# Norm factor applied behind the products: four MLPs, four FFNs and two cross-attention query products of a two-block network

## The chip, the cores and the metric

The kernel runs on one core of one Trainium2 chip. The metric is the device time of one launch in microseconds (us); lower is better. The engines are TensorE (PE in the rows, with its weight loads as PEld), VectorE (DVE), ScalarE (ACT), GpSimd (POOL) and SyncE (SP), which issues the weight transfers.

## The reference, cut to what matters

Every stage of the network starts with a norm of the residual x (256 tokens, 1024 channels) and ends by adding to x:

```
def rms_norm(x, g):                      # y = x * r * g, one factor r for each token
    y = x * lax.rsqrt(jnp.mean(x * x, axis=-1, keepdims=True) + 1e-6)
    return y * g

# block 1, four layers: mixer (gated delta rule, mLSTM, differential attention, gated delta rule), then
h = rms_norm(x, norm_g[i, 2])
x = x + rms_norm(jnp.square(jax.nn.relu(h @ w1)) @ w2, norm_g[i, 3])      # 1024 -> 4096 -> 1024

# block 2, two layers
x = x + 0.5 * swiglu(rms_norm(x, ffn1_norm), w_gate, w_up, w_down)        # 1024 -> 2816 -> 1024
x = x + hybrid_mixer(rms_norm(x, mix_norm), ...)
x = x + memory_cross_attention(rms_norm(x, cross_norm), rms_norm(mem, mem_norm), wq, wk, wv, wo)
x = x + 0.5 * swiglu(rms_norm(x, ffn2_norm), ...)
# swiglu(h) = (silu(h @ w_gate) * (h @ w_up)) @ w_down ; cross attention: q = h @ wq
```

## The kernel before

**Layout and products.** x is held transposed in xT (channels on partitions, 8 chunks of 128 channels by 256 tokens). All products are float32 made of three float32r products: an operand is split into a rounded high part and the rest as a low part, and high x high, high x low and low x high are summed in PSUM. Activations are split into hH and hL (the MLP's hidden ones into hidH and hidL), weights into wH and wL.

**Weights as slabs.** All weights come as 400 slabs of 1 MB (128 x 2048 float32) through a ring of 3 buffers. SP may load slab n when slab n-3 has its low part. ACT makes wH (`split`, L1058), DVE makes wL from it (L1495); there are two places for split slabs, so wH of slab n waits until the products of slab n-2 are done. A slab costs TensorE 48 matmuls of 256 columns (all at L459). On ACT, `ready(name, layer, j)` is the place in the queue where slab j+2 is split: it makes sure of the splits up to j+1, waits for the products of slab j, and splits slab j+2. On DVE `refill(name, layer, j)` makes wL up to slab j+2.

**Start of a stage.** DVE writes xT in four steps of two chunks (`post_norm`, L1534 and L1537, behind the four mixers of block 1 and its MLPs; `residual`, L1544, in block 2). ACT squares each step into sq (L1081), PE sums the squares over the channels with a matrix of ones (`norm_sum`, 8 matmuls in plain float32), ACT turns the sum into r by Ln and Exp (`rsqrt`, L1075 and L1076), DVE writes hT = x * g * r (L1506), ACT rounds it to hH (L1092), DVE makes hL (L1511), and `first_products` takes the stage's first two slabs together: for each pair of chunks of hH the first slab's high and low weights and the second slab's high weights, then hL, then the second slab's low weights. The third slab follows by `to_channels` or the loop in `ffn`. `ln_exp` (L1071) loads the activation table with Ln and Exp, at the head of ACT's part of a stage.

**The stages concerned.** `mlp` (4 times): 16 slabs of w1, each evacuated by ACT's Relu (L1141) and a DVE product of Relu and bank (L1560), split again to hidH and hidL, then 16 slabs of w2 and `post_norm`, which norms the product and adds it to x. `ffn` (4 times): 22 slabs with gate and up side by side; ACT's Silu of the gate half (L1159), DVE's product with the up half (L1582), hidH by ACT (L1154), hidL by DVE, then 11 slabs of w_down and `residual`. `cross` (2 times): 4 slabs of wq, evacuated by ACT's `channels` (L1121), while the memory is normed (in layer 0 with its own norm sum behind the third slab; the squares of the memory are L1414), then wk, wv, attention, wo.

The mlp stages and the first ffn start behind a `post_norm`, for which both slabs of the new stage have their wH already; the other five start behind a `residual`, where only the first slab has it, and ACT makes wH of the second slab behind the squares.

Of the kernel before, what the change touches and what calls it, by code (L numbers as in the profile page):

```python
# [15 lines left out]
P = 128  # L16
# [4 lines left out]
EPS = 1e-6  # L21
RING = 3
# [69 lines left out]

def schedule():
# [42 lines left out]

LAMBDA_INIT = 0.8 - 0.6 * math.exp(-0.3 * 2)


def program(nc, io, out, parts=None):  # L140
# [23 lines left out]
    with ExitStack() as ctx:  # L164
# [62 lines left out]
        with nc.sbuf_tensor("hidden_parts", [P, 2, 32, T], F32R) as hidden_parts:  # L227
            hidH, hidL = hidden_parts[:, 0, :, :], hidden_parts[:, 1, :, :]
        arena = sb("arena", [P, ARENA])
# [24 lines left out]
        prod_s = A.take(2 * 512, "p (b n) -> p b n", b=2)  # L254

# [36 lines left out]
        memH, memL = hidden_parts[:, 0, 24:32, :], hidden_parts[:, 1, 0:8, :]  # L292
        A = Arena(lay)
# [74 lines left out]
        def _(pool):  # L368
            scope[0] = ""
            W = Waits(pool, "pool_step")  # L370
            pool.memset(ones[:, :], 1.0)
            pool.memset(epsc[:, :], EPS).then_inc(sem("ones_set"), 1)
# [81 lines left out]
        def _(pe):  # L454
# [36 lines left out]
            def first_products(name, layer, js, c, at):  # L491
# [3 lines left out]
                high_w = [high(n[0], c), high(n[1], c)]  # L495
# [3 lines left out]
                def both_halves(b, w, x, k, ends=False):  # L499
                    for m in range(2):  # L500
                        ins = mm(ps[:, 4 + b, m * T:(m + 1) * T], at(w, k, m), x[:, k, :],
                                 w is high_w[b] and x is hH and k == 0 and m == 0, ends and k == DC - 1 and m == 1,
# [3 lines left out]
                for k0 in range(0, DC, 2):  # L506
                    pe.wait_ge(sem("hH_ready"), W.next("hH_ready"))
                    for b, w in ((0, high_w[0]), (0, low_w[0]), (1, high_w[1])):
                        for k in (k0, k0 + 1):
                            both_halves(b, w, hH, k)  # L510
                for k in range(DC):
                    if k % 2 == 0:
                        pe.wait_ge(sem("hL_ready"), W.next("hL_ready"))
                    last = both_halves(0, high_w[0], hL, k, ends=True)
                last.then_inc(sem("products_done"), 1)
                for k in range(DC):
                    both_halves(1, high_w[1], hL, k)
                pe.wait_ge(sem("low_split"), n[1] + 1)
                for k in range(DC):
                    last = both_halves(1, low_w[1], hH, k, ends=True)  # L520
# [29 lines left out]
            def norm_sum(bank=7):  # L550

                for c in range(4):
                    pe.wait_ge(sem("sq_ready"), W.next("sq_ready"))
                    for k in (2 * c, 2 * c + 1):
                        last = mm(ps[:, bank, 0:T], ones[:, 0:P], sq[:, k, :], k == 0, k == DC - 1)
                last.then_inc(sem("ss_ready"), 1)

# [28 lines left out]
            def down_product(name, layer, chunks, waited):  # L586

                for j in range(chunks // 2):
                    n = slab_no[(name, layer, j)]
# [17 lines left out]
            def mlp(i):  # L607
                norm_sum()
                first_products("mlp_w1", i, (0, 1), DC, columns)
                for j in range(2, 16):  # L610
                    to_channels("mlp_w1", i, j, bank_of(j), free="bank_read")
                down_product("mlp_w2", i, 32, range(0, 32, 2))
                pe.wait_ge(sem("bank_read"), W.next("bank_read", 4))
                norm_sum()

            def ffn(kind, l):
                norm_sum()
                first_products(kind, l, (0, 1), 2 * DC, lambda w, k, half: w[:, half * DC + k, :])
                for n in range(2, 22):
# [4 lines left out]
                    for half in range(2):  # L624
                        last = three(ps[:, 4 + n % 4, half * T:(half + 1) * T],
                                     [lambda k: wh[:, half * DC + k, :], lambda k: wl[:, half * DC + k, :]],
                                     [lambda k: hH[:, k, :], lambda k: hL[:, k, :]], DC,
# [325 lines left out]
            def cross(l):  # L953
                norm_sum()
# [4 lines left out]
                to_channels("cross_wq_2", l, 3, bank_of(3))  # L959
                pe.wait_ge(sem("mem_split"), W.next("mem_split", 4))  # L960
                for s in range(4):
                    pe.wait_ge(sem("evac"), W.next("evac"))
# [62 lines left out]
            pe.wait_ge(sem("lambda_ready"), W.next("lambda_ready"))  # L1025
            mm(ps[:, 1, 0:1], ones[0:1, 0:P], lwork[:, 130:131], True, True).then_inc(sem("lambda_spread"), 1)
            pe.wait_ge(sem("params_ready"), W.next("params_ready"))
# [7 lines left out]
            pe.wait_ge(sem("h_ready"), DC * (len(parts) + 1))  # L1035
# [8 lines left out]
        def _(act):  # L1044
# [28 lines left out]
            def rsqrt(src, dst, n, name):  # L1073

                W.chain(f(dst, src, ACT.Ln, scale=1.0 / n, bias=epsc[:, :]))  # L1075
                f(dst, dst, ACT.Exp, scale=-0.5).then_inc(sem(name), 1)  # L1076

            def norm(src, there, ahead):
# [5 lines left out]
                rsqrt(ps[:, 7, 0:T], rs[:, :], D, "rs_ready")  # L1084
# [8 lines left out]

            def split_mix(n):
# [5 lines left out]
            def post_norm(product):  # L1100

                norm(lambda c: two(ps[:, c, :]), lambda c: ready(*product(c), ahead=c < 3),
                     slab_no[product(3)[0:3]] + PARTS + 1)
# [33 lines left out]
            def mlp(i):  # L1137
                x_norm("mlp_w1", i)
# [6 lines left out]
                post_norm(lambda c: ("mlp_w2", i, 15, c))  # L1145
# [5 lines left out]
            def ffn(kind, l):  # L1151
                def hidden_high(n):
                    act.wait_ge(sem("bank_read"), W.next("bank_read"))
# [255 lines left out]
            def cross(l):  # L1409
                x_norm("cross_wq_2", l)  # L1410
# [5 lines left out]
                channels("cross_wq_2", l, 0, 4, chunks(qk, 0), scale=0.0625)  # L1416
# [7 lines left out]
                channels("cross_wq_2", l, 1, 6, chunks(qk, 4), scale=0.0625)  # L1424
# [38 lines left out]
            act.wait_ge(sem("lambda_sums"), W.next("lambda_sums"))  # L1463
            f(lwork[:, 130:132], lwork[:, 128:130], ACT.Exp).then_inc(sem("lambda_exp"), 1)
# [531 lines left out]
```

## Time and profile before

| | us |
|---|---|
| median of 3 runs | 3054.18 |
| the three runs | 3053.6, 3054.18, 3063.7 |
| the profiled execution | 3064.9 |
| its span in the trace | 3063.2 |
| mean granted TensorE clock in it | 0.967 of full speed |

Every engine runs its own queue in order; a row of a timeline is a start, a length, the engine and line, and in brackets how long the engine had been idle and who released it. Lengths of neighbouring instructions may overlap where the engine pipelines them. The profile gives TensorE's granted clock as a share of 2.4 GHz.

### The profile page before, as it was taken

The numbers are of one execution on the slowest core, as the hardware profiler recorded it, in microseconds if no ns is written. First come the engines' busy times: TensorE is split into PE (matmuls) and PEld (weight loads), VectorE is DVE, ScalarE is ACT, GpSimd is POOL, SyncE is SP. The second block draws the span as 40 slices with busy tenths as digits, with TensorE's granted clock in tenths as the row PEclk, the third lists the DMA queues.
The fourth block names the chain that finished last, engine by engine and source line by source line (L and its number), as shares of the span: only waits on it lengthen the run. The fifth ranks groups of instructions, "written<-read, shape, count | busy, mean of one in ns | idle before, by whom it ended". The sixth has DMA issues, their size and how long they took to land.

```text
span 3063.2 us, 50643 instructions
## 1 busy us (share of the span) xinstructions
PE 2857.0 (93%) x22666; PEld 2756.5 (90%) x22666; DVE 1671.9 (55%) x2004; ACT 1338.1 (44%) x1580; POOL 87.9 (3%) x98
## 2 busy tenths in 40 slices
PE   7998999889988999999999999899999999789998
PEld 7897998779987898988898999789999999789998
DVE  5675644356365554866554544744554544645553
ACT  3603534445345543531443444444443444444443
POOL 1300000000000000300000000000000000000000
PEclk8999999989999999999999999999999999899999
DMA  6401554326532454510454765324565664225563
GB/s 188 142 16 42 187 185 138 110 83 193 188 129 83 152 186 144 160 62 1 147 191 145 193 193 159 117 69 152 152 187 166 184 193 154 94 76 172 145 196 114
DMA packets 426633, 427.97 MB, mean 140 GB/s; under 512 B 8274, under 2 KB 397760, under 8 KB 426288
## 3 DMA queue, kind: packets, MB, share of 16 engines
q1 hardware_dynamic: 426064, 424.37, 44.2%
q8 instruction: 179, 2.93, 0.4%
q0 software_dynamic: 352, 0.36, 0.1%
q14 instruction: 38, 0.31, 0.0%
HBM read 423.65 MB, written 1.05 MB: 139 GB/s over the span
## 4 chain that ended last, share of the span: by engine, by line
PE 88%; ACT 5%; DVE 4%; issue 1%; DMA 0%; SPq 0%; POOL 0%; ACTq 0%; DVEq 0%; POOLq 0%
PE ps L459 88%; ACT wH L1058 1%; DVE wL L1495 1%; DVE hT L1506 1%; DVE sq L1534 0%; ACT rs L1075 0%; DVE xT L1537 0%; DVE sq L1597 0%; ACT rs L1076 0%; ACT hH L1092 0%; ACT sq L1081 0%; DVE hT L1600 0%; DMA ring<-in_gdn_w_in 0%; PE ps L840 0%; ACT L1071 0%
## 5 line engine op out<-in xcount | busy, mean ns | idle before, releaser
L1495 DVE TENSOR_TENSOR wL<-ring,wH 128x2048 fp32r<-128x2048 f32 x400 | 916.7, 2292 | 1003.8 <-ACT wH L1058 1003.5
L1058 ACT ACTIVATE wH<-ring 128x2048 fp32r<-128x2048 f32 x400 | 767.2, 1918 | 1251.5 <-PE ps L459 1235.4
L459 PE MATMUL ps<-hH,wH 128*128 128x256 f32 x4160 | 599.6, 287 | 56.9 <-ACT hH L1092 42.9
L459 PE MATMUL ps<-hidden_parts,wH 128*128 128x256 f32 x3712 | 643.7, 280 | 1.2 <-ACT wH L1058 1.2
L459 PEld LDWEIGHTS ps<-hH,wH 128*128 128x128 f32 x4160 | 540.0, 195 | 76.0 <-issue 71.1
L459 PE MATMUL ps<-hH,wL 128*128 128x256 f32 x4160 | 575.5, 281 | 1.6 <-DVE wL L1495 1.6
L459 PEld LDWEIGHTS ps<-hidden_parts,wH 128*128 128x128 f32 x3712 | 558.6, 188 | 1.4 <-DVE hidden_parts L1905 1.4
L459 PE MATMUL ps<-hL,wH 128*128 128x256 f32 x4160 | 559.9, 279 | 0.0
L459 PEld LDWEIGHTS ps<-hH,wL 128*128 128x128 f32 x4160 | 527.9, 192 | 1.8 <-DVE wL L1495 1.8
L459 PEld LDWEIGHTS ps<-hL,wH 128*128 128x128 f32 x4160 | 517.8, 190 | 0.0
L459 PE MATMUL ps<-hidden_parts,wL 128*128 128x256 f32 x1856 | 499.9, 279 | 0.1
L459 PE MATMUL ps<-arena 128*128 128x128 f32 (+1 forms) x2288 | 337.9, 304 | 66.7 <-DVE arena L1854 30.4
L459 PEld LDWEIGHTS ps<-arena 128*128 128x128 f32 x2288 | 303.6, 199 | 86.3 <-issue 19.4
L459 PEld LDWEIGHTS ps<-hidden_parts,wL 128*128 128x128 f32 x1856 | 339.8, 187 | 0.3 <-DVE wL L1495 0.3
L459 PE MATMUL ps<-sq,ones 128*128 128x256 f32 (+1 forms) x488 | 153.8, 469 | 49.9 <-ACT sq L1081 33.9
L459 PEld LDWEIGHTS ps<-sq,ones 128*128 128x128 f32 x488 | 101.4, 217 | 87.2 <-ACT sq L1081 34.7
L1109 ACT ACTIVATE sq<-ps 128x512 f32<-128x512 f32 x12 | 7.2, 597 | 191.7 <-PE ps L459 191.7
L1689 DVE TENSOR_TENSOR arena<-arena,ps 128x512 f32<-128x512 f32 x104 | 67.2, 685 | 33.2 <-PE ps L459 33.2
L1506 DVE SCALAR_TENSOR_TENSOR hT<-xT,vec,rs 128x256 f32<-128x256 f32 x136 | 55.4, 480 | 53.6 <-ACT rs L1076 53.6
L1081 ACT ACTIVATE sq<-xT 128x512 f32<-128x512 f32 x68 | 41.8, 629 | 43.9 <-DVE xT L1537 24.2
L1644 DVE SCALAR_TENSOR_TENSOR arena<-arena 128x256 f32<-128x256 f32 x144 | 60.1, 483 | 0.0
L459 PE MATMUL ps<-arena,const 128*128 128x256 f32 (+2 forms) x176 | 53.8, 395 | 5.0 <-DVE arena L1731 4.3
(240 smaller groups left out, 1806.8 us busy)
## 6 DMA issues: line engine op xcount, KB each, us to landing
ring<-in_mlp_w SPq DMA_DIRECT2D x128, 1024.0 KB, 5.3
ring<-in_ffn_w_gate SPq DMA_DIRECT2D x88, 512.0 KB, 3.9
ring<-in_ffn_w_up SPq DMA_DIRECT2D x88, 512.0 KB, 5.2
ring<-in_ffn_w_down SPq DMA_DIRECT2D x44, 1024.0 KB, 4.8
ring<-in_gdn_w_in SPq DMA_DIRECT2D x32, 1024.0 KB, 5.8
ring<-in_w_in SPq DMA_DIRECT2D x28, 1024.0 KB, 5.2
ring<-in_mlstm_w_in SPq DMA_DIRECT2D x12, 1024.0 KB, 5.2
ring<-in_diff_w_in SPq DMA_DIRECT2D x12, 1024.0 KB, 5.1
```

Source lines behind the costliest of these rows:

```text
L459: return pe.matmul(o, l, r, start=start, stop=stop, **k)
L1058: f(wH[:, n % PARTS, :], ring[:, n % RING, :], ACT.Copy).then_inc(sem("high_split"), 1)
L1081: f(sq[:, 2 * c:2 * c + 2, :], src(c), ACT.Square).then_inc(sem("sq_ready"), 1)
L1109: f(sq[:, 2 * b:2 * b + 2, :], src(b), ACT.Square).then_inc(sem("sq_ready"), 1)
L1495: tt(wL[:, n % PARTS, :], ring[:, n % RING, :], wH[:, n % PARTS, :].bitcast(F32), ALU.subtract)\
L1506: stt(hT[:, c, :], xT[:, c, :], column(gain, k0 + c), rs[:, :], ALU.mult, ALU.mult)\
L1644: ins = stt(dst, src, w, dst, ALU.mult, ALU.add)
L1689: ins = tt(v, v, ps[:, bank, :].rearrange("p (h n) -> p h n", h=4), ALU.subtract)
```

## The change

Ten stages (4 mlp, 4 ffn, 2 cross) no longer form hT. With gain g, ACT writes the high part straight from x (Copy with scale g), DVE the low part x * g - high, and the products are of x * g. The token factor r is put in behind them:

- `mlp`: nothing is scaled, since relu(r a)^2 = r^2 relu(a)^2 and the norm behind the MLP takes the common factor out; its epsilon becomes eps / r^4, which is added to the norm sum by one more matmul of ones with a tile rs that ACT makes by one Square of the sum (`norm_floor`, run before the third w2 slab).
- `ffn`: DVE multiplies the whole bank (gate and up) by r into act_s; Silu then reads act_s, one slab later, and a second DVE product makes prod_s; hidH follows two slabs later.
- `cross`: DVE evacuates the query banks with r and the factor 0.0625 in place of ACT.
- The squares, the norm sum (bank 2) and r come behind the first two slabs. In the first of the ffn stages and in mlp the squares lie between the copies, in the others behind the split of the second slab. In the three instances of `ffn` and the two of `cross` behind a `residual`, `first_products` waits for the second slab's high weights only when it reaches them (`together=False`).
- Aside: setup semaphores are merged; one small memset is added.

```diff
 def first_products(..., src=(hH, hL), together=True):          # PE
     for k0 in range(0, DC, 2):
         pe.wait_ge(sem("hH_ready"), W.next("hH_ready"))
-        for b, w in ((0, high_w[0]), (0, low_w[0]), (1, high_w[1])):
-            for k in (k0, k0 + 1):
-                both_halves(b, w, hH, k)
+        for k in (k0, k0 + 1):
+            both_halves(0, high_w[0], xH, k, start=True)
+        for k in (k0, k0 + 1):
+            both_halves(0, low_w[0], xH, k)
+        for k in (k0, k0 + 1) if together else ():
+            both_halves(1, high_w[1], xH, k, start=True)
+    if not together:
+        high_w.append(high(n[1], c))
+        for k in range(DC):
+            both_halves(1, high_w[1], xH, k, start=True)
...
+def norm_floor(bank=7):
+    pe.wait_ge(sem("floor_set"), W.next("floor_set"))
+    mm(ps[:, bank, 0:T], ones[:, 0:P], rs[:, :], True, False, skip_group_check=True)
...
 def mlp(i):                                                    # PE
-    norm_sum()
     first_products("mlp_w1", i, (0, 1), DC, columns)
+    norm_sum(2)
...
 def cross(l):                                                  # PE; ffn likewise
-    norm_sum()
-    first_products("cross_wq_2", l, (0, 1), DC, columns)
-    to_channels("cross_wq_2", l, 2, bank_of(2))
+    first_products("cross_wq_2", l, (0, 1), DC, columns, src=cross_x, together=False)
+    norm_sum(2)
+    to_channels("cross_wq_2", l, 2, bank_of(2), src=cross_x)
...
+def late_norm(name, layer, gain, k0, x_parts, between):        # ACT
+    def square(c):
+        f(sq[:, 2 * c:2 * c + 2, :], xT[:, 2 * c:2 * c + 2, :], ACT.Square).then_inc(sem("sq_ready"), 1)
+    for c in range(4):
+        act.wait_ge(sem("x_ready"), W.next("x_ready"))
+        for k in (2 * c, 2 * c + 1):
+            ins = f(x_parts[0][:, k, :], xT[:, k, :], ACT.Copy, scale=column(gain, k0 + k))
+        ins.then_inc(sem("hH_ready"), 1)
+        if between:
+            square(c)
+    split(slab_no[(name, layer, 0)] + PARTS)
+    for c in range(0 if between else 4):
+        square(c)
+    act.wait_ge(sem("ss_ready"), W.next("ss_ready"))
...
 def mlp(i):                                                    # ACT
-    x_norm("mlp_w1", i)
+    late_norm("mlp_w1", i, "norm_g", (4 * i + 2) * DC, (hH, hL), True)
+    f(rs[:, :], ps[:, 2, 0:T], ACT.Square, scale=FLOOR / D, bias=bcast[:, 36:37])\
+        .then_inc(sem("floor_set"), 1)
...
 def ffn(kind, l):                                              # ACT
-    x_norm(kind, l)
+    late_norm(kind, l, f"{kind}_norm_2", l * DC, ffn_x, (kind, l) == ("ffn1", 0))
+    ln_exp()
+    rsqrt(ps[:, 2, 0:T], rs[:, :], D, "rs_ready")
     for n in range(22):
         ready(kind, l, n)
-        f(act_s[:, n % 2, 0:T], ps[:, 4 + n % 4, 0:T], ACT.Silu).then_inc(sem("act_ready"), 1)
         if n >= 1:
-            hidden_high(n - 1)
+            gate_unit(n - 1)
+        if n >= 2:
+            hidden_high(n - 2)
...
 def cross(l):                                                  # ACT
-    x_norm("cross_wq_2", l)
+    late_norm("cross_wq_2", l, "cross_norm_2", l * DC, cross_x, False)
+    ln_exp()
+    rsqrt(ps[:, 2, 0:T], rs[:, :], D, "rs_ready")
     if l == 0:
         for c in range(4):
             f(sq[:, 2 * c:2 * c + 2, :], memT[:, 2 * c:2 * c + 2, :], ACT.Square)\
                 .then_inc(sem("sq_ready"), 1)
-    channels("cross_wq_2", l, 0, 4, chunks(qk, 0), scale=0.0625)
+    ready("cross_wq_2", l, 0)
+    ready("cross_wq_2", l, 1)
...
+def late_low(gain, k0, x_parts, name, layer):                  # DVE
+    for c in range(4):
+        dve.wait_ge(sem("hH_ready"), W.next("hH_ready"))
+        for k in (2 * c, 2 * c + 1):
+            ins = stt(x_parts[1][:, k, :], xT[:, k, :], column(gain, k0 + k),
+                      x_parts[0][:, k, :].bitcast(F32), ALU.mult, ALU.subtract)
+        ins.then_inc(sem("hL_ready"), 1)
+    split(slab_no[(name, layer, 0)] + PARTS)
...
     for n in range(22):                                        # DVE, ffn
         refill(kind, l, n)
+        if n == 0:
+            dve.wait_ge(sem("rs_ready"), W.next("rs_ready"))
...
-        dve.wait_ge(sem("act_ready"), W.next("act_ready"))
-        tt(prod_s[:, n % 2, 0:T], act_s[:, n % 2, 0:T], ps[:, 4 + n % 4, T:2 * T], ALU.mult)\
+        dve.wait_ge(sem("products_done"), group(kind, l, n))
+        tt(two(act_s[:, n % 2, :]), two(ps[:, 4 + n % 4, :]), rs_twice(), ALU.mult)\
             .then_inc(sem("bank_read"), 1)
...
+            unit(n - 1)
+        if n >= 2:
+            hidden_low(n - 2)
...
+    def query(g):                                              # DVE, cross; between refills of wq
+        stt(qk[:, 2 * g:2 * g + 2, :], two(ps[:, 4 + g, :]), 0.0625, rs_twice(), ALU.mult, ALU.mult)\
+            .then_inc(sem("q_evac"), 1)
```

## Rows read from the trace of the kernel before

**Rows 1.** The page: busy time of each engine, and the chain that ended last.
```profile
PE 2857.0 (93%) x22666; PEld 2756.5 (90%) x22666; DVE 1671.9 (55%) x2004; ACT 1338.1 (44%) x1580; POOL 87.9 (3%) x98
...
PE 88%; ACT 5%; DVE 4%; issue 1%; DMA 0%; SPq 0%; POOL 0%; ACTq 0%; DVEq 0%; POOLq 0%
```

**Rows 2.** Timeline, entry of the third ffn (start us, length us, engine, line).
```profile
2356.34 2.48 DVE L1544 SCALAR_TENSOR_TENSOR xT<-ps,xT 128x512 f32<-128x512 f32 x4
...
2357.46 0.28 PE L459 MATMUL ps<-hidden_parts,wL 128*128 128x256 f32 x1
...
2357.84 3.69 PE L459 MATMUL ps<-sq,ones 128*128 128x256 f32 x16
...
2361.57 0.47 ACT L1075 ACTIVATE rs<-ps,epsc 128x256 f32<-128x256 f32 x1 [0.28 <-PE ps L459]
...
2362.52 3.26 DVE L1506 SCALAR_TENSOR_TENSOR hT<-xT,vec,rs 128x256 f32<-128x256 f32 x8 [3.70 <-ACT rs L1076]
...
2364.21 1.08 PE L459 MATMUL ps<-hH,wH 128*128 128x256 f32 x4 [2.69 <-ACT hH L1092]
...
2373.64 1.92 ACT L1058 ACTIVATE wH<-ring 128x2048 fp32r<-128x2048 f32 x1 [7.20 <-PE ps L459]
...
2375.57 1.28 ACT L1159 ACT_TABLE_LOAD   x1
2375.59 2.29 DVE L1495 TENSOR_TENSOR wL<-ring,wH 128x2048 fp32r<-128x2048 f32 x1 [5.20 <-ACT wH L1058]
2376.87 0.39 ACT L1159 ACTIVATE arena<-ps 128x256 f32<-128x256 f32 x1
...
2377.13 1.11 PE L459 MATMUL ps<-hH,wH 128*128 128x256 f32 x8
```

**Rows 3.** Timeline, entries of the first cross and the last ffn.
```profile
2042.46 1.07 PE L459 MATMUL ps<-hH,wL 128*128 128x256 f32 x8
...
2052.30 2.17 ACT L1414 ACTIVATE sq<-memT 128x512 f32<-128x512 f32 x4
...
2062.72 1.07 PE L459 MATMUL ps<-hH,wH 128*128 128x256 f32 x8
...
2856.51 1.07 PE L459 MATMUL ps<-hH,wL 128*128 128x256 f32 x8
...
2875.18 1.07 PE L459 MATMUL ps<-hH,wH 128*128 128x256 f32 x8
```

**Rows 4.** Timeline, entries of the first mlp and the first ffn.
```profile
291.85 0.88 DVE L1534 SCALAR_TENSOR_TENSOR sq<-ps,vec,rs 128x256 f32<-128x256 f32 x2 [5.52 <-ACT rs L1076]
...
297.30 0.69 DVE L1537 TENSOR_TENSOR xT<-xT,sq 128x512 f32<-128x512 f32 x1
...
315.40 1.07 PE L459 MATMUL ps<-hH,wH 128*128 128x256 f32 x8
...
1667.56 0.88 DVE L1534 SCALAR_TENSOR_TENSOR sq<-ps,vec,rs 128x256 f32<-128x256 f32 x2 [5.76 <-ACT rs L1076]
...
1691.04 1.07 PE L459 MATMUL ps<-hH,wH 128*128 128x256 f32 x8
```

**Rows 5.** Two neighbouring ACT instructions in a steady ffn slab.
```profile
2384.89 0.37 ACT L1159 ACTIVATE arena<-ps 128x256 f32<-128x256 f32 x1
...
2385.15 0.41 ACT L1154 ACTIVATE hidden_parts<-arena 128x256 fp32r<-128x256 f32 x1
```

**Rows 6.** Windows: us, length, busy PE, PEld, DVE, ACT, POOL; granted clock; DMA.
```profile
2364.20:2366.00 1.80, 1.79 (x9) 1.80 (x10) 1.80 (x5) 1.45 (x3) 0.00 (x0) 0.54 0.00 0
...
2745.00:2748.00 3.00, 0.32 (x2) 0.03 (x1) 1.68 (x5) 1.66 (x4) 0.00 (x0) 1.00 0.00 0
2748.00:2750.00 2.00, 1.99 (x17) 2.00 (x18) 2.00 (x5) 1.66 (x3) 0.00 (x0) 1.00 0.00 0
```

**Rows 7.** Windows inside the products of two ffn stages, same columns.
```profile
1720.00:1760.00 40.00, 40.00 (x355) 40.00 (x355) 22.17 (x22) 18.52 (x24) 0.00 (x0) 1.00 0.73 200
...
2200.00:2240.00 40.00, 40.00 (x342) 40.00 (x341) 20.71 (x21) 17.85 (x22) 0.00 (x0) 1.00 0.68 188
```

More of the change, by code:

```diff
@@ L21 @@
 EPS = 1e-6
+FLOOR = math.sqrt(EPS * D / P)
 RING = 3
@@ L90 @@
 LAYERS2 = 2
+LATE = ("mlp", "ffn1", "ffn2", "cross")
 def schedule():
@@ L254, in program @@
         prod_s = A.take(2 * 512, "p (b n) -> p b n", b=2)
+        gate_s = A.take(2 * T, "p (b n) -> p b n", b=2)
         A = Arena()
@@ L292, in program @@
         memH, memL = hidden_parts[:, 0, 24:32, :], hidden_parts[:, 1, 0:8, :]
+        ffn_x = (hidH[:, 24:32, :], hidL[:, 24:32, :])
+        cross_x = [flat_parts[:, at:at + DC * T].rearrange("p (c t) -> p c t", c=DC)
+                   for at in (after_pair, after_pair + DC * T)]
         A = Arena(lay)
@@ L489, in bank_of, with first_products, both_halves @@
                 return 4 + j % 4
[L491 removed]
+            def first_products(name, layer, js, c, at, src=(hH, hL), together=True):
                 n = [slab_no[(name, layer, j)] for j in js]
[L495 removed]
+                xH, xL = src
+                high_w = [high(n[0], c)] + ([high(n[1], c)] if together else [])
                 low_w = [low(n[0], c), low(n[1], c)]
                 pe.wait_ge(sem("low_split"), n[0] + 1)
[L499 removed]
+                def both_halves(b, w, x, k, start=False, ends=False):
                     for m in range(2):
                         ins = mm(ps[:, 4 + b, m * T:(m + 1) * T], at(w, k, m), x[:, k, :],
[L502 removed]
+                                 start and k == 0 and m == 0, ends and k == DC - 1 and m == 1,
                                  skip_group_check=True)
@@ L548, in to_tokens, with norm_sum @@
                 last.then_inc(sem("products_done"), 1)
-            def norm_sum(bank=7):
+            def norm_sum(bank=7, on_floor=False):
                 for c in range(4):
@@ L554, in norm_sum @@
                     for k in (2 * c, 2 * c + 1):
-                        last = mm(ps[:, bank, 0:T], ones[:, 0:P], sq[:, k, :], k == 0, k == DC - 1)
+                        last = mm(ps[:, bank, 0:T], ones[:, 0:P], sq[:, k, :], k == 0 and not on_floor, k == DC - 1,
+                                  skip_group_check=on_floor)
                 last.then_inc(sem("ss_ready"), 1)
+            def norm_floor(bank=7):
+                pe.wait_ge(sem("floor_set"), W.next("floor_set"))
+                mm(ps[:, bank, 0:T], ones[:, 0:P], rs[:, :], True, False, skip_group_check=True)
             def head_sums(n):
@@ L1034, in _ @@
             norm_sum()
-            pe.wait_ge(sem("h_ready"), DC * (len(parts) + 1))
+            pe.wait_ge(sem("h_ready"), DC * (sum(kind not in LATE for kind, _ in parts) + 1))
             for t in range(TT):
@@ L1071, in ln_exp, with rsqrt, norm @@
                 act.preload_act_table_set("natural_log_exp_and_others")
-            def rsqrt(src, dst, n, name):
-                W.chain(f(dst, src, ACT.Ln, scale=1.0 / n, bias=epsc[:, :]))
+            def rsqrt(src, dst, n, name, bias=None):
+                W.chain(f(dst, src, ACT.Ln, scale=1.0 / n, bias=epsc[:, :] if bias is None else bias))
                 f(dst, dst, ACT.Exp, scale=-0.5).then_inc(sem(name), 1)
-            def norm(src, there, ahead):
+            def norm(src, there, ahead, bias=None):
                 for c in range(4):
@@ L1144, in mlp @@
                 hidden_high(15)
-                post_norm(lambda c: ("mlp_w2", i, 15, c))
+                post_norm(lambda c: ("mlp_w2", i, 15, c), 0.0)
             def hidden_high(g):
@@ L1423, in cross @@
                         .then_inc(sem("memH_ready"), 1)
-                channels("cross_wq_2", l, 1, 6, chunks(qk, 4), scale=0.0625)
+                ready("cross_wq_2", l, 2)
+                ready("cross_wq_2", l, 3)
                 channels("cross_wk_2", l, 0, 4, chunks(qk, 8))
```

112 lines of the change are left out of this document (74 added, 38 removed).

## The prediction

> **What bounds the kernel now.** I read the page first: TensorE is busy 93% of the span and makes 88% of the chain that ended last [rows 1]. Inside a stage only fewer or faster matmuls could help; what a reordering can win lies at the entries of stages, so I went to the timeline there.
>
> Entry behind a `residual` [rows 2]: the last product ends at 2357.74 (2357.46 + 0.28). The norm sum follows at once and takes 3.7. TensorE then stands for 2.7, while ACT makes r (2361.57 to 2362.52), DVE hT and ACT hH. The first matmul starts at 2364.21, the third slab at 2377.13. I count from the last product's end to the third slab's first matmul, because from there on nothing of the entry is left: 19.4 here, 19.2 for the first cross, 17.6 for the last ffn [rows 3], 92.2 over the five entries of this kind.
>
> Entry behind a `post_norm` [rows 4]: DVE writes x in four steps of 1.5, from a = 291.85 to 297.99 (297.30 + 0.69); the third slab starts at a + 23.55, in the first ffn 23.48 after its own a (1691.04 - 1667.56).
>
> Last, the windows: behind the idle 2.7 the granted clock was 0.54, of the lower of its two levels (1.2 against 2.4 GHz); at another entry with like idleness it stayed 1.00 [rows 6].
>
> **What the change takes away.** The entry loses r, hT and the wait for them: after the first copies TensorE can start. The norm sum isn't taken away, only moved.
>
> **What it adds: the third slab is late.** Before, ACT makes wH of the third slab as soon as the first slab's products are done: 2373.64, well ahead of its use at 2377.13 [rows 2]. In the new queue that split stands in `ready(..., 0)`, behind `late_norm`, whose last instruction waits for the norm sum, and TensorE gives that only after both first slabs. So TensorE ends the norm sum and has nothing split: it waits for ACT's remaining chain and then for a whole wH. Queued behind that ACT wait are the activation table load (ffn and cross), Ln and Exp (in mlp one Square), in the first cross four squares of the memory as well, and only then the splits. Before, the table load ran while TensorE was still in the old stage; now it is on the path.
>
> *Five entries behind a residual.* Time from the last product's end. The first step of x is there before that end (DVE starts at 2356.34, four steps take 2.48 [rows 2]); two ACT copies of 256 columns follow at a pace of 0.26 [rows 5], so TensorE starts at about +0.25. The last step of hH is there at about +2.0, ahead of TensorE's 0.95 for a step (8 matmuls), and wH of the second slab (1.92) at +3.9, when TensorE wants it at +4.1. Two slabs are 96 matmuls of 0.117 (40 us over 342 [rows 7]): 11.3. The sum takes 3.6. That is +15.15. Then table load 1.28, Ln and Exp 0.95, wH 1.92 [rows 2], and some 0.05 of handover: +19.35. DVE's wL (2.29) is started by the end of wH, and TensorE has only 16 matmuls (1.87) in front of the low weights: another 0.45. A standstill of 4.2 is longer than the 2.7 that already lowered the clock in some entries. For the price of the low clock I take 1.3 (19.4 against 18.0, which is what the 92.2 leave for each of the two entries not shown, whose clock stayed full, gives 1.4; part of the slow stretch can fall into the standstill). Together 21.1, five times 105.5: **+13.3** against 92.2.
>
> *First cross.* The memory's squares, 2.17 [rows 3], formerly in ACT's slack, lie before the third slab's split: **+2.2**. DVE also takes over four evacuations (0.6 each, by L1544's pace) between wL splits, which makes wL of the first wk slab late by 0.2 to 0.4: **+0.5** for both cross stages.
>
> *Four mlp.* x comes at the pace of `post_norm`: the first hH at a + 2.35, the last at a + 6.85 (297.99, then two copies). A step holds 12 matmuls (1.4), less than the pace of 1.5, so a + 8.25; 48 matmuls more, 5.5; the norm sum 3.6: a + 17.3. Square and wH: 2.45, no table load here. The wait for wL 0.45. Low clock at the start (TensorE has stood for over 3, as before) 1.4, after the gap of 2.5 half of that, 0.7. The added matmul of ones 0.45 (an eighth of the sum). In all 22.75 against 23.55, taken for all four: **-3.2**.
>
> *First ffn.* The same to a + 17.3, plus 1.4 at the low clock, 4.2 for table, Ln, Exp, wH, then 0.45 and 1.3: 24.65 against 23.5, **+1.2**.
>
> *What costs nothing.* DVE's low parts are eight instructions at 0.4 (3.26 [rows 2]), done by +5.3, wanted at +7.8; behind them wL of the second slab ends at +7.6, wanted at +9.6. Without that cover each late microsecond would stop TensorE. In a steady ffn slab DVE gets one 512-column instruction where it had 256 columns, and one of 256 more: 2.29 + 0.6 + 0.4 + 0.4 = 3.7 of the slab's 5.4 to 5.7 (48 matmuls). ACT keeps its three. Banks are read about 5 after their products; TensorE wants them three slabs later. DVE waits for r at the first ffn slab behind wL of the third slab, so that the one queued behind is wL of the fourth, wanted over 6 later. SP's loads hang on wL: the ones for the fifth slab are issued at about +7.6, wanted at +31. Even the end of the up phase (Silu, product, hidH in turn after the last bank) is over 6.4 after its products, and w_down's third slab is wanted at 11.3.
>
> The sum: 13.3 + 2.2 + 0.5 - 3.2 + 1.2 = **+14.0** on the profiled execution's 3064.9 gives 3079. That execution lies 10.7 above the median of the runs shown. I put the same difference on the median 3054.2: **3068**.
>
> **A page's rule against the row.** From the table load's start to the start of Silu are 1.30 (2375.57 to 2376.87), and the instruction before ended as it began [rows 2]; nothing stands between. The Trainium skill (ScalarE: Activation LUTs, What ACT_TABLE_LOAD costs) adds about 1.38 of drain to the 1.28. By it six entries would cost 8.3 more, by the row none; it is a rival below.
>
> **Bounds of what the trace doesn't show.** An ACT copy with a pointer as scale: 0.26 a piece or, unpipelined, 0.41; even then a step (0.82) is under TensorE's 0.95: 0 either way. The low clock: nothing at all in any entry is -10.6 (six times 1.3, four times 0.7); 1.8 (19.4 against 17.6) in all ten is +7.4. The pace of matmuls: the profile holds two at full clock, 0.1127 and 0.1170 (355 and 342 in 40 us [rows 7]), and a stage keeps the one that it starts with. In an ffn's 20 later slabs the difference is 4.1, in an mlp's 14 it is 2.9, in cross 2.1. Four of the ten stages ran slow in this execution, so new starts may give from -13 to +19; I take zero.
>
> **The rivals.**
> 1. *The forecast*: entries a little dearer behind residuals, a little cheaper in mlp. 3068, own range 3058 to 3079. Chance 0.55.
> 2. *The pace decides*: starts behind a low clock mostly gave the fast pace in the profile, and the new standstills make more of those. With all ten fast, +14 - 13: 3055, no change. For it: the 10 us between the runs shown are about two ffn stages' worth; against it: the median may hold the fast ones already. 0.20.
> 3. *The table switch drains ACT* on the exposed path: +14 + 8.3, 3076. Against it the 1.30 above. (The page above has this rule.) 0.08.
> 4. *The ffn slab gets bound by the ACT-DVE handovers*: bank, Silu, product, hidH, hidL, five in turn. It decides only if a slab's turn passes 5.4; at 0.3 over, 80 slabs are +24, so 3092. Against it 3.7 of 5.4. 0.05.
> 5. *The other side: the third slab isn't late*. If its wH were made before ACT waits for the sum, an entry behind a residual would be 15.2 + no standstill against 18.4, five times -3.2, an mlp some -3.6 to -4.3, the first ffn -4.7: about -37, 3017; it decides faster from half of that on. Nothing in ACT's order allows it, except that I misread the order. 0.07; the rest, 0.05, is spread.
>
> **How the numbers follow.** A measurement of this kernel tells about 0.5%, 15 us, from no change. 3068 is 0.45% above 3054, so the forecast's own range straddles that bound (3069.5): about 0.22 of its 0.55 lies above. With rivals 3 and 4 and a share of the spread: slower 0.38. Faster: rival 5 and little else, 0.08. Same: 0.54. The range of 8 in 10 reaches to rivals 2 and 3 and takes in most of the bounds of pace and clock: 3050 to 3082.
>
> **What the changed profile would show.** Right: TensorE idle for 4.2 in front of the third slab of every ffn and cross, over 6 in the first cross, about 2.5 in mlp, released by ACT's wH; a table load between the norm sum's end and Ln; first matmul within 0.3 of the last product; third slab at +19.8 or more. Wrong: a wH of the third slab ahead of Ln; idle TensorE inside the ffn's up phase; a first step that waits for ACT's copies. What makes the number wrong though the steps are right is the pace of the matmuls per stage, to be read from counts in 40 us.

## The result and the profile after

The changed kernel takes **3091.96 us** (median of 4 runs, 3086.32 to 3095.29); the kernel before, beside it, 3055.19. The ratio is 1.0116, 95% interval 1.0098 to 1.0134: slower by 1.2%, beyond the predicted range of 3050 to 3082. The profiled execution took 3094.05, its span is 3092.3, the mean granted clock 0.964.

The page of the changed kernel, busy time and the chain that ended last (against [rows 1]):
```profile
PE 2874.7 (93%) x22674; PEld 2774.8 (90%) x22674; DVE 1712.1 (55%) x2060; ACT 1334.8 (43%) x1604; POOL 88.2 (3%) x99
...
PE 87%; ACT 7%; DVE 4%; issue 1%; DMA 0%; POOL 0%; SPq 0%; ACTq 0%; DVEq 0%; POOLq 0%
```
ACT's share of the chain went from 5% to 7%: the new standstills. But TensorE is also busy 17.7 us longer, with eight matmuls more.

The entry of the second ffn stage (ffn2, layer 0; of the kind of [rows 2]), timeline of the changed kernel:
```profile
2176.94 2.48 DVE L1621 SCALAR_TENSOR_TENSOR xT<-ps,xT 128x512 f32<-128x512 f32 x4
2177.05 1.07 PE L471 MATMUL ps<-hH,wL 128*128 128x256 f32 x8
2177.66 3.31 ACT L1135 ACTIVATE hidden_parts<-xT,vec 128x256 fp32r<-128x256 f32 x8 [2.96 <-DVE xT L1621]
2178.71 0.70 PE L471 MATMUL ps<-hidden_parts,wH 128*128 128x256 f32 x4 [0.59 <-ACT hidden_parts L1135]
...
2180.88 1.91 ACT L1091 ACTIVATE wH<-ring 128x2048 fp32r<-128x2048 f32 x1
...
2182.84 5.92 PE L471 MATMUL ps<-hidden_parts,wH 128*128 128x256 f32 x48 [0.26 <-ACT wH L1091]
...
2190.48 3.62 PE L471 MATMUL ps<-sq,ones 128*128 128x256 f32 x16
...
2194.12 1.28 ACT L1104 ACT_TABLE_LOAD   x1 [9.26 <-PE ps L471]
2195.42 0.47 ACT L1108 ACTIVATE rs<-ps,epsc 128x256 f32<-128x256 f32 x1
...
2196.25 3.69 ACT L1091 ACTIVATE wH<-ring 128x2048 fp32r<-128x2048 f32 x2
...
2198.17 2.29 DVE L1560 TENSOR_TENSOR wL<-ring,wH 128x2048 fp32r<-128x2048 f32 x1 [13.06 <-ACT wH L1091]
2198.19 3.78 PE L471 MATMUL ps<-hidden_parts,wH 128*128 128x256 f32 x16 [4.09 <-ACT wH L1091]
...
2201.77 1.67 PE L471 MATMUL ps<-hidden_parts,wL 128*128 128x256 f32 x8
...
2203.28 1.98 PE L471 MATMUL ps<-hidden_parts,wH 128*128 128x256 f32 x16
```
Read it from the row at 2198.19 upward. The third slab starts at 2198.19 after 4.09 idle, released by ACT's wH, which stands behind Ln and Exp, which stand behind the table load, which waited 9.26 for the norm sum. This is the standstill that the prediction described. The old stage ends at 2178.12 (2177.05 + 1.07), so the third slab comes at +20.07. The standstill is the same in both profiles of the changed kernel: 4.09 or 4.10 in the four ffn and the second cross, 6.17 in the first cross, 2.36 or 2.37 in the four mlp.

The clock in the same place (windows of the changed kernel, columns as in [rows 6]):
```profile
2194.10:2198.20 4.10, 0.01 (x1) 0.01 (x1) 0.03 (x1) 4.03 (x5) 0.00 (x0) 0.76 0.00 0
2198.20:2200.20 2.00, 2.00 (x9) 2.00 (x10) 2.00 (x1) 1.98 (x2) 0.00 (x0) 0.50 0.00 0
2200.20:2203.20 3.00, 3.00 (x17) 3.00 (x16) 2.97 (x3) 1.46 (x2) 0.00 (x0) 0.53 0.44 126
```
TensorE comes back at about half clock, the lower of its two levels (1.2 GHz against 2.4). By the timeline above, 24 matmuls (16 and 8) take 5.1, from 2198.19 to 2203.28, where they take 2.8 at full clock (0.115 each). (The counts of two neighbouring windows share the matmuls on their border.)

The first cross and the first mlp, timeline of the changed kernel:
```profile
2073.15 3.75 PE L471 MATMUL ps<-hidden_parts,wH 128*128 128x256 f32 x16 [6.17 <-ACT wH L1091]
...
288.25 0.88 DVE L1611 SCALAR_TENSOR_TENSOR sq<-ps,vec,rs 128x256 f32<-128x256 f32 x2 [5.74 <-ACT rs L1109]
...
307.19 0.47 ACT L1189 ACTIVATE rs<-ps,bcast 128x256 f32<-128x256 f32 x1 [11.34 <-PE ps L471]
...
309.51 1.19 PE L471 MATMUL ps<-hH,wH 128*128 128x256 f32 x8 [2.36 <-ACT wH L1091]
```
Standstills of 6.17 and 2.36, predicted "over 6" and "about 2.5".

The pace of matmuls in four ffn stages, windows of the changed kernel (against [rows 7]):
```profile
1740.00:1780.00 40.00, 40.00 (x342) 40.00 (x341) 25.64 (x29) 18.13 (x23) 0.00 (x0) 1.00 0.69 188
2240.00:2280.00 40.00, 40.00 (x355) 40.00 (x354) 26.61 (x29) 19.22 (x24) 0.00 (x0) 1.00 0.71 197
2440.00:2480.00 40.00, 40.00 (x342) 40.00 (x342) 25.95 (x29) 18.13 (x24) 0.00 (x0) 1.00 0.68 185
2940.00:2980.00 40.00, 40.00 (x342) 40.00 (x341) 25.57 (x28) 18.17 (x22) 0.00 (x0) 1.00 0.68 186
```
The clock is full in all four, TensorE has no gap, and yet three make 342 matmuls where one makes 355. I call these the slow and the quick pace; per slab of 48 they are 5.654 and 5.440 us (the distance of neighbouring wH splits), so a slow ffn costs 20 x 0.214 = 4.3, a slow mlp 14 x 0.214 = 3.0. In the profile of before two ffn and one mlp are slow (11.5), in this one three ffn and two mlp (18.8).

This holds for the first products of a stage alone. The second ones (w_down, w2), whose moving operand is always in hidden_parts, run at the slow pace in all eight ffn and mlp stages of all sixteen profiles of this study, 128 of 128, also behind quick first products. In the kernel before, the stage that is quick at 1720 in [rows 7], in its w_down products:
```profile
1800.00:1840.00 40.00, 40.00 (x342) 40.00 (x342) 17.14 (x10) 14.75 (x11) 0.00 (x0) 1.00 0.55 185
```
Below, a slow or a quick stage means its first products.

To see where the time went I cut both traces at ACT's wH splits: an *entry* goes from the last but one slab of the old stage to the fifth of the new one, a *body* from there to the next entry. For the ten changed stages the entries are 20.9 longer and the bodies 8.7; the stages whose code is unchanged add 3.8, and the first mixer, ahead of all of them, is shorter by some 4. Together that is the difference of the two spans, 29.1.

### The profile page after: what moved, and what is told of

Its sections match the earlier page's. It is cut to its first block, busy times and chain, and to the rows that moved or that the text cites. A ratio compares the mean times of both kernels' runs of the same rounds, so it can differ in the third digit from the quotient of the medians.

```text
span 3092.3 us, 50833 instructions
## 1 busy us (share of the span) xinstructions
PE 2874.7 (93%) x22674; PEld 2774.8 (90%) x22674; DVE 1712.1 (55%) x2060; ACT 1334.8 (43%) x1604; POOL 88.2 (3%) x99
## 4 chain that ended last, share of the span: by engine, by line
PE 87%; ACT 7%; DVE 4%; issue 1%; DMA 0%; POOL 0%; SPq 0%; ACTq 0%; DVEq 0%; POOLq 0%
PE ps L471 87%; ACT wH L1091 2%; DVE wL L1560 1%; ACT hidden_parts L1135 1%; ACT L1104 0%; DVE sq L1690 0%; DVE sq L1611 0%; ACT rs L1108 0%; DVE hT L1693 0%; DVE xT L1614 0%; DMA ring<-in_gdn_w_in 0%; DVE hT L1571 0%; PE ps L873 0%; ACT rs L1109 0%; ACT arena L1287 0%
## 5 line engine op out<-in xcount | busy, mean ns | idle before, releaser
L471 PE MATMUL ps<-hidden_parts,wH 128*128 128x256 f32 x6784 | 1046.8, 281 | 34.9 <-ACT wH L1091 28.1
L471 PEld LDWEIGHTS ps<-hidden_parts,wH 128*128 128x128 f32 x6784 | 941.3, 190 | 40.0 <-ACT wH L1091 30.8
L471 PE MATMUL ps<-hidden_parts,wL 128*128 128x256 f32 x3392 | 715.1, 280 | 0.1
L471 PEld LDWEIGHTS ps<-hidden_parts,wL 128*128 128x128 f32 x3392 | 537.3, 189 | 0.3 <-DVE wL L1560 0.3
L471 PE MATMUL ps<-hH,wH 128*128 128x256 f32 x2624 | 389.2, 292 | 53.1 <-ACT hH L1125 16.1
L471 PEld LDWEIGHTS ps<-hH,wH 128*128 128x128 f32 x2624 | 348.0, 198 | 70.7 <-issue 55.4
L471 PE MATMUL ps<-hH,wL 128*128 128x256 f32 x2624 | 366.7, 283 | 2.1 <-DVE wL L1560 2.1
L471 PE MATMUL ps<-hL,wH 128*128 128x256 f32 x2624 | 354.7, 280 | 0.0
L471 PEld LDWEIGHTS ps<-hH,wL 128*128 128x128 f32 x2624 | 336.4, 193 | 2.7 <-DVE wL L1560 2.7
L471 PEld LDWEIGHTS ps<-hL,wH 128*128 128x128 f32 x2624 | 328.3, 191 | 0.0
```

Of the source, the lines that this page charges most:

```text
L471: return pe.matmul(o, l, r, start=start, stop=stop, **k)
```

## The experiments

### Both kernels once more

Edit: none; one execution each of the changed kernel and of the kernel before, taken at different times.

> The changed kernel once more, for a second profile. Theory A (the pace of the matmuls is drawn anew at each stage's start, in each execution): the stages that run at 0.113 us a matmul are other ones than in the first profile (there the first and third mlp and the second ffn), and the time differs from 3094 by up to 10 us. Theory B (the pace belongs to the program, by where its instructions lie): the same stages are fast. Time 3084 to 3096 either way.

> The kernel before once more, for a second profile of the pace of its stages. Theory (the pace is drawn at each start, and hH gives both): other stages slow than in the first profile (there the third mlp, ffn2 of layer 0 and ffn1 of layer 1), 1 to 5 of 8 in all, time 3047 to 3075. Rival (fixed by the program): the same three.

Measured: 3091.15 and 3048.86. The entries differ by 19.5, as in the first pair (20.9). The bodies differ by 17.2 instead of 8.7, the stages of unchanged code by 0.9, and the first mixer, whose code is unchanged, is 4.6 longer where it had been 4 shorter. All four ffn are now slow and no mlp is; in the kernel before one mlp alone is slow. So the entries belong to the program, and the pace of a stage can change from one execution of the same program to the next. The kernel before, the same stages in its second profile:
```profile
1720.00:1760.00 40.00, 40.00 (x355) 40.00 (x355) 22.64 (x23) 17.61 (x22) 0.00 (x0) 1.00 0.72 195
...
2220.00:2260.00 40.00, 40.00 (x355) 40.00 (x354) 22.63 (x22) 17.91 (x23) 0.00 (x0) 1.00 0.72 197
2420.00:2460.00 40.00, 40.00 (x356) 40.00 (x355) 21.67 (x22) 19.00 (x24) 0.00 (x0) 1.00 0.73 205
2910.00:2950.00 40.00, 40.00 (x355) 40.00 (x355) 22.17 (x22) 18.51 (x24) 0.00 (x0) 1.00 0.73 199
```
The stage around 2220, slow in [rows 7], is quick here. This draw is also most of the spread between profiled executions: the seven profiles in the order of before (this kernel twice, and the two variants further down that only move the activations, five times) took 3049 to 3075. Less 4.3 for each slow ffn and 3.0 for each slow mlp they lie at 3046 to 3053. By the same reckoning the two profiles of the changed kernel lie at 3074 and 3075. The kernel before took 3047 to 3076 over all its runs but one (4145); its medians were 3055 to 3064 in the four series of several runs, so each version is judged by its ratio to the runs of the kernel before beside it. Beside the changed kernel's 3091.15 here, the median of 18 runs of the kernel before was 3062.57: 28.6 apart, where the first series had 36.8.

### The third slab's high weights ahead of the wait

```diff
 def late_norm(...):                                            # ACT
     ...
+    ready(name, layer, 0)
     act.wait_ge(sem("ss_ready"), W.next("ss_ready"))
```

> ACT splits the third slab's high part before it waits for the norm sum, nothing else. Theory (the third slab is late, as predicted): the standstills of 4.2 in six entries and 2.4 in four go, with the waits for the low part and the low clock behind them: 6 x 5.9 + 2.2 + 4 x 3.6, about 52 us less than the changed kernel, 3040. Rival (most of the loss lies in the longer handover of the ffn slabs or in the pace of the matmuls): less than 20 us of the 37 come back, 3072 or more.

Measured: 3045.84 (8 runs), ratio to before 0.9957 (0.9938 to 0.9975): 46 us below the changed kernel's median, and 45 below its second profiled execution (3091.15), which was taken beside these runs. The same ffn entry, timeline of this kernel:
```profile
2151.82 1.91 ACT L1091 ACTIVATE wH<-ring 128x2048 fp32r<-128x2048 f32 x1
...
2157.94 1.92 ACT L1091 ACTIVATE wH<-ring 128x2048 fp32r<-128x2048 f32 x1 [2.13 <-PE ps L471]
...
2161.43 3.61 PE L471 MATMUL ps<-sq,ones 128*128 128x256 f32 x16
...
2164.69 2.23 PE L471 MATMUL ps<-hidden_parts,wH 128*128 128x256 f32 x16
2165.07 1.28 ACT L1104 ACT_TABLE_LOAD   x1 [5.21 <-PE ps L471]
```
The split at 2157.94 stands ahead of the norm sum, TensorE passes from the sum to the third slab with no idle time in brackets, and the table load runs beside it. The clock of this kernel there:
```profile
2161.40:2164.70 3.30, 3.30 (x19) 2.91 (x17) 0.79 (x1) 0.00 (x0) 0.00 (x0) 1.00 0.33 94
2164.70:2166.70 2.00, 2.00 (x18) 1.97 (x17) 0.00 (x0) 1.62 (x2) 0.00 (x0) 1.00 1.17 322
```
Standstill and low clock are gone together, and no entry of the ten has a standstill in front of its third slab any more. The ten entries are 51 shorter than in the changed kernel, 31 shorter than before. What follows: the order of one split is the whole loss at the entries. But 31 were won there against the kernel before and only 17 arrived in the median: all four ffn and three mlp are slow in this profile, and the bodies are 22 longer than in the second profile of before. With every slow stage taken out at 4.3 and 3.0, the five profiles of kernels with the third slab early lie at 3014 to 3025, against the 3046 to 3053 above: there the 31 are seen again.

### The table load ahead of the norm sum

```diff
 def ffn(kind, l):                                              # ACT, cross likewise
+    ln_exp()
     late_norm(...)
-    ln_exp()
```

> The changed kernel with the table load of ffn and cross moved back to the head of the stage. Theory: six times 1.28 off the standstill, nothing else: 3084. Rival (the switch drains the engine as well, 1.38 each): 3076. Rival (the low clock decides, a shorter standstill keeps it high in some entries): 3078 to 3082.

Measured: 3083.18 (5 runs), ratio 1.0067 (1.0039 to 1.0094). The table load lies in the old stage, and Ln starts behind the sum at once; timeline of this kernel:
```profile
2173.09 1.28 ACT L1104 ACT_TABLE_LOAD   x1
...
2192.50 0.47 ACT L1108 ACTIVATE rs<-ps,epsc 128x256 f32<-128x256 f32 x1 [9.27 <-PE ps L471]
...
2195.28 2.08 PE L471 MATMUL ps<-hidden_parts,wH 128*128 128x256 f32 x8 [2.81 <-ACT wH L1091]
```
The standstill is 2.81 instead of 4.09, exactly the 1.28 of the load (2.81 in all four ffn and the second cross, 4.89 instead of 6.17 in the first cross). The entries are 11.4 shorter than in the two profiles of the changed kernel (473.2 against a mean of 484.6): six loads of 1.28 are 7.7. The other 3.7 lie mostly behind the standstills: over the ten entries the first 72 matmuls from the third slab on are late by 15.6 against their stage's pace, and by 17.1 and 20.6 in the two profiles of the changed kernel. That time at the low clock differs as much between two profiles of one kernel, so it isn't a gain to count on.

### The mlp stages alone

```diff
-LATE = ("mlp", "ffn1", "ffn2", "cross")
+LATE = ("mlp",)                            # ffn and cross as in the kernel before
```

> Only the four mlp stages changed, ffn and cross as before. Theory: the mlp entries are about even (in the two profiles their sum is -0.5), so 3053 to 3059, no change from before. Rival (anything in the new entries spoils the pace of the matmuls behind them, 2.9 in an mlp): up to 3067.

Measured: 3062.41 (10 runs) against 3062.57 of the kernel before beside it, ratio 0.9992 (0.9972 to 1.0012): no change that can be told. The entries of the ten stages are 1.8 shorter than before (predicted 3.2), and all four ffn, which again read hH, are quick.

### The kernel before, with the ffn's activations in hidden_parts

The change does one more thing, which the prediction had not priced: the ffn's x * g lies in the last quarter of hidden_parts (`ffn_x`) instead of hH and hL. This experiment moves only that, with the norm and the order of before.

```diff
+ffn_x = (hidden_parts[:, 0, 24:32, :], hidden_parts[:, 1, 24:32, :])
...
-    for k in (k0, k0 + 1): both_halves(b, w, hH, k)            # likewise all reads and writes of hH, hL in ffn
+    for k in (k0, k0 + 1): both_halves(b, w, src[0], k)
```

> The kernel before with one edit: the ffn's split activations lie in the spare chunks 24 to 31 of hidden_parts, where the changed kernel has them, in place of hH and hL; no order is changed. So far an ffn's up phase ran slow (0.1177 us a matmul) in 11 of 12 stages that read hidden_parts and in 2 of 8 that read hH. Theory (the place of the moving operand decides how often a stage is slow): all four ffn stages slow here, up to 4.5 each against a fast one, some 5 to 12 above the kernel before. Rival (the new order of the entry decides): the four ffn stages are as mixed as before, same time.

(The count in the expectation should be 15 of 16 stages: three of four in the first profile of the changed kernel, four of four in its second and in those of the two experiments.) Measured: 3073.32 (10 runs), ratio 1.0045 (1.0022 to 1.0069), 14 us by the medians. All four ffn are slow in the profile, with 342 matmuls in each window; the first and the last:
```profile
1720.00:1760.00 40.00, 40.00 (x342) 40.00 (x341) 21.13 (x22) 17.43 (x21) 0.00 (x0) 1.00 0.67 185
...
2910.00:2950.00 40.00, 40.00 (x342) 40.00 (x341) 20.71 (x21) 17.86 (x22) 0.00 (x0) 1.00 0.69 188
```
The same kernel again:

> Second profile of before_in_hidden. Theory (without the shift slow nearly always): all four ffn stages slow, 3063 or more. Rival (mixed as with the shift): one or more fast.

Measured: 3069.76, all four ffn slow again (the one run of the kernel before beside it took 3068.23, so this pair of times alone tells nothing). Nothing in this kernel stands still longer than before (the entries agree within 1 us). Moving the activations is enough to make the stages slow.

### Third slab early, with ffn1 back in hH and hL

```diff
+ffn_at = {"ffn1": (hH, hL), "ffn2": (hidH[:, 24:32, :], hidL[:, 24:32, :])}     # with the edit of third_early
```

> The kernel third_early with the activations of the two ffn1 stages back in hH and hL (ffn2 stays in hidden_parts, since hH is still read there when it starts). Theory (place): ffn1 mostly fast, ffn2 slow in the same execution, 3 to 9 below third_early's 3046: 3037 to 3043. Rival (the order of the entry): no difference between ffn1 and ffn2, 3046.

> Second profile of early_ffn1_moved, whose two ffn1 stages read hH and were slow in its first profile. Theory (hH is fast in most stages, old order or new): at least one of the two fast. Rival (the new order of the entry keeps them slow): both slow again.

Measured: 3049.39 (10 runs), ratio 0.9965 (0.9944 to 0.9986), and 3050.87 in the second execution. The theory missed: both ffn1 stages read hH and are slow in both profiles, four of four. In the second one even all eight mlp and ffn stages are. So the place isn't all. These two stages differ from those of before in the order of the entry and in the slab's handovers; no run here separates the two.

### Both edits of the order

```diff
+    ln_exp()                     # ahead of late_norm, in ffn and cross
     late_norm(...)               # with ready(name, layer, 0) ahead of its wait
```

> Both repairs: the third slab split before the wait for the norm sum, and the table load at the head of the stage. Theory (with the third slab early, table load, Ln and Exp lie beside TensorE's work on that slab): no gain over third_early, 3043 to 3049. Rival (the factor r is late for DVE's first bank and that holds the fourth slab): up to 8 less than third_early.

Measured: 3044.48 (10 runs), ratio 0.9951 (0.9928 to 0.9974), entries 432.5 against 433.6. With the third slab early, the table load is covered.

### The activations elsewhere in hidden_parts

```diff
+ffn_x = [hidden_parts.rearrange("p a c t -> p (a c t)")[:, at:at + DC * T].rearrange("p (c t) -> p c t", c=DC)
+         for at in (22 * T + 32, 54 * T + 32)]
```

Both parts start 480 columns, 1920 bytes, lower than before: not at chunk 24 but 32 columns (128 bytes) behind the start of chunk 22. I call this the shifted place.

Once in the kernel before (`before_hidden_shifted`), once in `third_early` (`early_shifted`).

> The kernel before_in_hidden with the same activations in the same tensor, but from chunk 22 plus 32 columns on: their addresses then have the remainder by 512 bytes that hH and hL have (128), where chunk 24 has 0. Theory (the remainder of the moving operand's address decides): the four ffn stages are mixed again, in 1 to 3 of 4 fast, and the time returns from 3073 to that of the kernel before, 3057 to 3064. Rival (hidden_parts itself, or its distance from the weights, decides): all four slow, 3068 to 3078.

> third_early with the same shift of the ffn activations. Theory (remainder): 1 to 3 of the 4 ffn stages fast, 3037 to 3042 against third_early's 3046. Rival (the new order of the entry keeps an ffn slow by itself, as the two ffn1 stages of early_ffn1_moved were though they read hH): all four slow, 3043 to 3049.

Measured: 3058.64 (10 runs), ratio 0.9991 (0.9969 to 1.0012), and 3043.45 (9 runs), ratio 0.9934 (0.9916 to 0.9951). The loss of the unshifted place (1.0045) is gone. Yet the first profile of the kernel before with the shifted place has all four ffn slow, so it was run twice more:

> Second profile of before_hidden_shifted, whose first profile had all four ffn stages slow (3067.5) while its ten times reach down to 3051.6. Theory (the shift makes the pace mixed, the first profile was a slow draw): at least one ffn stage fast and a time under 3062 when two or more are. Rival (ffn stages that read hidden_parts are always slow, and the spread comes from elsewhere): all four slow again.

> Third profile of before_hidden_shifted, same expectations as for the second.

Measured: 3060.65 and 3061.43. Two ffn are slow in the second profile, one in the third, both taken side by side on one chip, so the chip does not fix which; the third has three slow mlp besides. Windows of the second:
```profile
1720.00:1760.00 40.00, 40.00 (x355) 40.00 (x355) 21.16 (x22) 19.42 (x24) 0.00 (x0) 1.00 0.73 200
2220.00:2260.00 40.00, 40.00 (x355) 40.00 (x354) 21.52 (x24) 18.09 (x22) 0.00 (x0) 1.00 0.69 187
2420.00:2460.00 40.00, 40.00 (x342) 40.00 (x341) 20.71 (x21) 17.88 (x22) 0.00 (x0) 1.00 0.69 189
```
Seven of twelve are slow over the three profiles. In `early_shifted` all four ffn are slow in its one profile. It is the best version of this study, faster than the kernel before by 0.7% (0.5% by the nearer bound of its interval), but its interval overlaps that of `third_early`, so what the shift itself brings there isn't settled.

The stages counted over all profiles:

| ffn stages | slow | of |
|---|---|---|
| order of before, reading hH | 2 | 12 |
| order of before, shifted place | 7 | 12 |
| any order, hidden_parts unshifted | 31 | 32 |
| third slab early, shifted place | 4 | 4 |
| third slab early, reading hH | 4 | 4 |

| mlp stages (all read hH) | slow | of |
|---|---|---|
| order of before | 7 | 28 |
| new order, with the standstill | 5 | 16 |
| new order, third slab early | 16 | 20 |

## Why the prediction was wrong

**The step that failed: "I take zero" for the pace of the matmuls.** The prediction had seen both paces and gave their bounds (-13 to +19), but took the draw to be the same before and after. It is not. The change moves the ffn's activations (`ffn_x` in place of hH and hL), which the prediction passed over, and from the new place 31 of 32 stages ran slow, against 2 of 12 from the old one. By these shares 3.2 of the four ffn stages more are slow, 14 us, and 14 us is what the move cost alone in the kernel before (1.0045). Of the 24 us between 3068 and 3092 that is more than half. In the two pairs of profiles the slow stages make 6.8 and 13.5 of the 8.7 and 17.2 by which the bodies got longer: a slow ffn's body is 4.06 longer than a quick one's, a slow mlp's 2.78. Each mlp body is 0.43 longer at equal pace, 1.7 in all, about what the prediction priced the added matmul of ones at (0.45). "A stage keeps the one that it starts with" also holds only up to its second products, which are always slow.

**The entries: right in mechanism, too small in size.** Predicted +14.0, measured +20.9 and +19.5, 6 more. The true miss is 8, since 1.8 of the prediction's mlp term are the added matmuls of ones, which lie in the bodies. By kind, mean of both pairs:

| | predicted | measured |
|---|---|---|
| four mlp | -3.2 (without the matmuls of ones -5.0) | -2.5 |
| first ffn | +1.2 | +2.3 |
| first cross | about +4.4 | +6.0 |
| the four others behind a residual, together | +11.6 | +14.5 |

In the first mlp the third slab starts 21.26 behind DVE's first step (309.51 - 288.25), where the prediction's terms give 21.15. In the ffn entry shown above, with the prediction's terms:
- First matmul "at about +0.25": at +0.59. ACT's copies with a pointer as scale don't overlap, 8 take 3.31, 0.41 each, the upper bound that the text held harmless. It was harmless for each step, but not for the first, nor for the wH of the second slab behind the eight: ready at +4.67 (2180.88 + 1.91), said +3.9, and TensorE waits 0.26. The end of the sum comes at +15.98 instead of +15.15.
- The standstill: 4.2 predicted, 4.09 measured.
- The low clock: 1.3 taken, 2.3 measured (24 matmuls in 5.1 instead of 2.8). Behind the five standstills of 4.09 or 4.10 in each of the two profiles the next 72 matmuls are late by 1.5 to 2.7 against their stage's pace, in the mean by 2.2.
- The wait for the low weights, priced at 0.45, did not come: at the lower clock the 16 matmuls took 3.78, longer than the 2.29 of wL. Together with the low clock that is 2.3 where the prediction had 1.75.

**What was right.** The late third slab and its place, the idle times of 4.2, over 6 and 2.5, the table load between the sum and Ln, and the sign. *What costs nothing* held: in a steady ffn slab of the changed kernel
```profile
2300.72 2.29 DVE L1560 TENSOR_TENSOR wL<-ring,wH 128x2048 fp32r<-128x2048 f32 x1 [1.75 <-ACT wH L1091]
...
2302.93 0.68 DVE L1666 TENSOR_TENSOR arena<-ps,rs 128x512 f32<-128x512 f32 x1
...
2303.65 0.43 DVE L1651 TENSOR_TENSOR arena<-arena 128x256 f32<-128x256 f32 x1
...
2303.99 0.42 DVE L1656 TENSOR_TENSOR hidden_parts<-arena,hidden_parts 128x256 fp32r<-128x256 f32 x1
...
2306.16 2.29 DVE L1560 TENSOR_TENSOR wL<-ring,wH 128x2048 fp32r<-128x2048 f32 x1 [1.75 <-ACT wH L1091]
```
DVE's round of 3.7 repeats every 5.44 and waits 1.75 in each.

**The rivals.** *The pace decides* was the right rival with the wrong sign: the standstills did not bring quick stages (5 of 16 mlp slow with them, 7 of 28 in the order of before). *The ffn slab gets bound by handovers* would give 3092, which is the measured time, but falls by the slab just shown: a stage with the new handovers ran at the quick 5.44, and the kernel of before in hidden_parts is slow with the old ones. *The table switch drains ACT* falls too: from the start of the load to the start of Ln are 1.30 (2194.12 to 2195.42), and `table_ahead` shortened this standstill by 1.28. The Trainium skill (ScalarE: Activation LUTs, What ACT_TABLE_LOAD costs) adds about 1.38 of drain; this trace doesn't show it, and here the measurement decides. *The third slab isn't late* was right as to price within 6, once it was built: -31 at the entries for the -37 named.

**What stays open.** Why a place, and a start without standstill, make stages slow. By the addresses of the built programs, which no trace here shows, hH and hL start at a remainder of 128 bytes modulo 512, the unshifted quarter of hidden_parts at 0, the shifted place at 128. Equal remainders gave 2 of 12 and 7 of 12 in the order of before, too few stages to tell those two apart, and 8 of 8 with the third slab early, so a remainder alone does not decide. The shift also moved the operand by 1920 bytes; no other place and no moved weights were tried. That the second products, which read hidden_parts too, were slow 128 times of 128 fits the place, but those products differ in more than that. For ffn stages that read hH, 4 of 4 slow against 2 of 12, the new handovers may count as well as the order. The reading that the third slab early makes mlp stages slow (16 of 20 against 12 of 44 in the other orders) rests on counts alone, and no run separates it from what else starts earlier there.

## What to carry to other kernels

When an in-order engine makes something that the critical engine needs next, and a wait for that critical engine is put ahead of it, both stand still: read the queue behind every new wait for what is wanted first, and put that ahead (here one line, 46 us). A tensor that is merely moved is a change of its own: try it alone in the old kernel before the rest is built on it. Where the time of a stage is drawn anew in each execution, compare counts of stages over several profiles, since a single pair can show half or double the effect.

## What the runs showed of the hardware

- Matmuls of 256 columns with a weight load each have two steady paces at full granted clock, 355 or 342 in 40 us, each kept through a stage's first products. Which one can change from execution to execution of the same program, and the odds went with where the moving operand lies (2 of 12 slow against 31 of 32 in ffn) and, by counts alone, with the order of the stage's entry (mlp 12 of 44 slow against 16 of 20).
- The w_down and w2 products, with the moving operand in hidden_parts, ran at 342 in 40 us in 128 of 128 cases, whatever the pace of the products ahead of them.
- After 4.09 idle at the entry of ffn2, layer 0, the granted clock was 0.50 and 0.53 for 5.0 us; with no idle time at the same entry it stayed at 1.00.
- ACT copies of 128x256 from SBUF with a pointer as scale took 0.41 each, without the overlap that lets neighbours in [rows 5] start every 0.26.
- A table load delayed the next ACT instruction by 1.30, 0.02 more than its own 1.28.
